# Seven block products instead of eight for an FFN down projection, with the operand sums made on VectorE

## The reference, cut to what matters

```python
hf = rmsnorm(x, norm_ffn_g)
x = x + (jax.nn.silu(hf @ w_gate) * (hf @ w_up)) @ w_down   # w_down: 2816 x 1024
...
return rmsnorm(x, norm_final_g)
```

## Time and profile before

| | |
|---|---|
| runs | 1137.77 us median of 3 (1137.57 to 1142.76) |
| profiled execution | 1141.42 us, span from first to last instruction 1139.6 us |
| busy share of the span | PE 98%, VectorE 62%, ScalarE 51%, GpSimd 13% |
| granted TensorE clock | 0.996 of full speed over the span |
| chain that ended last | PE 83% of the span |
| DMA | 193.96 MB, mean 170 GB/s |

### The profile page before, as it was taken

How to read it: one execution, slowest core, us unless ns; L and a number is a source line. 1 busy time by engine, 2 the same in 40 slices (tenths; PEclk the granted TensorE clock), 3 DMA queues, 4 the chain that set the end, 5 groups by cost and what they waited for, 6 DMA issues and landing times.

```text
span 1139.6 us, 17781 instructions
## 1 busy us (share of the span) xinstructions
PE 1112.0 (98%) x7033; PEld 984.8 (86%) x7033; DVE 707.6 (62%) x997; ACT 583.6 (51%) x767; POOL 142.6 (13%) x105
## 2 busy tenths in 40 slices
PE   8899999999998999999999999999999999999997
PEld 7767888888887888888888999898899989999996
DVE  5764565565668646565656878566587566554554
ACT  5565544444579554444455546455555346443443
POOL 3543300000265240000030000000000011000001
PEclk9999999999999999999999999999999999999999
DMA  7917565555442236556545654436643545656552
GB/s 216 306 54 186 182 198 188 200 190 184 118 137 88 98 111 222 191 186 201 189 156 185 204 171 149 132 128 223 203 159 120 185 148 160 221 175 194 189 172 89
DMA packets 138782, 193.96 MB, mean 170 GB/s; under 512 B 7147, under 2 KB 112840, under 8 KB 138716
## 3 DMA queue, kind: packets, MB, share of 16 engines
q1 hardware_dynamic: 126796, 181.92, 48.4%
q10 hardware_dynamic: 11312, 11.05, 3.6%
q0 software_dynamic: 608, 0.08, 0.1%
HBM read 191.90 MB, written 6.37 MB: 174 GB/s over the span
## 4 chain that ended last, share of the span: by engine, by line
PE 83%; ACT 6%; DVE 5%; issue 2%; DMA 2%; POOL 0%; ACTq 0%; DVEq 0%; POOLq 0%
PE psum L548 20%; PE psum L549 20%; PE psum L550 20%; PE psum L709 11%; PE psum L710 5%; ACT arena L1552 3%; PE psum L637 2%; ACT whi L1566 2%; DVE wlo L2125 1%; DMA raw<-in_a_w_in 1%; PE psum L1264 1%; PE psum L668 1%; PE psum L1237 1%; DVE arena L2566 1%; DMA raw<-in_b_w_o 0%
## 5 line engine op out<-in xcount | busy, mean ns | idle before, releaser
L1566 ACT ACTIVATE whi<-raw 128x2048 fp32r<-128x2048 f32 (+2 forms) x174 | 325.9, 1875 | 255.5 <-PE psum L550 172.5
L2125 DVE TENSOR_TENSOR wlo<-raw,whi 128x2048 fp32r<-128x2048 f32 (+1 forms) x149 | 337.5, 2267 | 184.1 <-ACT whi L1566 183.2
L548 PE MATMUL psum<-xA,whi 128*128 128x256 f32 x840 | 239.8, 285 | 2.7 <-DVE wlo L2125 1.7
L549 PE MATMUL psum<-xA,whi 128*128 128x256 f32 x840 | 237.6, 283 | 0.0
L550 PE MATMUL psum<-xA,wlo 128*128 128x256 f32 x840 | 237.5, 283 | 0.0
L1535 POOL TENSOR_TENSOR wlo<-raw,whi 128x288 fp32r<-128x288 f32 (+3 forms) x56 | 112.6, 2037 | 793.8 <-ACT whi L1566 793.5
L709 PE MATMUL psum<-xA,whi 128*128 128x512 f32 x512 | 183.0, 400 | 0.0
L548 PEld LDWEIGHTS psum<-xA,whi 128*128 128x128 f32 x840 | 160.3, 191 | 6.0 <-DVE wlo L2125 3.2
L549 PEld LDWEIGHTS psum<-xA,whi 128*128 128x128 f32 x840 | 160.4, 191 | 0.7
L550 PEld LDWEIGHTS psum<-xA,wlo 128*128 128x128 f32 x840 | 160.4, 191 | 0.1
L548 PE MATMUL psum<-whi,xC 128*128 128x512 f32 (+1 forms) x384 | 149.2, 389 | 1.1 <-DVE xC L2439 1.1
(11 more groups left out here) (269 smaller groups left out, 1339.7 us busy)
## 6 DMA issues: line engine op xcount, KB each, us to landing
raw<-in_w_in SPq DMA_DIRECT2D x42, 1024.0 KB, 4.9
raw<-in_mlp_w_up SPq DMA_DIRECT2D x32, 1024.0 KB, 5.4
raw<-in_mlp_w_down SPq DMA_DIRECT2D x32, 1024.0 KB, 4.8
raw<-in_w_gate SPq DMA_DIRECT2D x11, 1024.0 KB, 5.1
raw<-in_w_up SPq DMA_DIRECT2D x11, 1024.0 KB, 5.2
raw<-in_w_down SPq DMA_DIRECT2D x11, 1024.0 KB, 4.8
raw<-in_a_w_in SPq DMA_DIRECT2D x6, 1024.0 KB, 7.1
raw<-in_a_w_o SPq DMA_DIRECT2D x4, 1024.0 KB, 4.7
```

Source lines behind the costliest of these rows:

```text
L548: nc.tensor.matmul(out, lh, rh, start=start, stop=False, skip_group_check=skip)
L549: nc.tensor.matmul(out, lh, rl, start=False, stop=False, skip_group_check=skip)
L1566: nc.scalar.activation(whi[c % N_SPLIT][:, 0:n], raw[c % N_RAW][:, 0:n], ACT.Copy).then_inc(hi_sem, 1)
L2125: V.tensor_tensor(wlo[c % N_SPLIT][:, 0:n], raw[c % N_RAW][:, 0:n], f(whi[c % N_SPLIT][:, 0:n]), ALU.subtract).then_inc(lo_sem["dve"], 1)
```

## The change

The eight block products of d_0 to d_9 become seven products of sums (the scheme of Strassen and Winograd); d_10 keeps its eight. The MLPs of the first two layers stay as they are.

- **Operands.** VectorE makes four sums of the down weights (`wsum`, 4 × 512 columns) and four of the hidden features (4 × 128). With the three weight blocks that are used plain, the weights' high and low parts are 7 × 512 = 3584 columns a turn, in buffers of their own (`down_split`, two turns' worth); the hidden features' are 7 × 128 = 896. The weight sums of d_{p+1} are made in turn p, "a turn ahead".
- **Buffers.** d chunks leave the ring of `raw` buffers and have two of their own (`down_raw` and a part of `arena`). g and u chunks alternate in the two `raw` buffers. The loading order is unchanged, but d0 is loaded earlier, behind the last chunk of the layer before, and each d load waits for the low part of the d chunk two before.
- **Banks.** M1, M5, M6 and M7 collect in banks 4 to 7, M2, M3, M4 in banks 3, 2, 1. Gate and up sums both use bank 0 from g2 on, so g_{p+1} waits for the product of turn p and u_{p+1} for the scaled gate of p+1.
- **Order on TensorE.** g_{p+1}; M1, M6, M7; u_{p+1}; M5, M2, M3, M4.
- **The end.** `seven_sums` puts M1 and M5 to M7 together into `hres`, before `residual_add`.

The core of the diff:

```diff
@@ PE
-            def ffn_down(c, lo_count, h_count, j2, start, last):
-                ...
+            def seven_products(s, p, order, loop=None, start=False, closing=None, part=None):
+                ...
+                if part in (None, 0):
+                    pe.wait_ge(down_low_raw, count(lambda x: whole_count(s, x)))
+                    pe.wait_ge(down_low_sum, count(lambda x: sums_count(s, x)))
+                    pe.wait_ge(hidden_low, count(lambda x: whole_count(s, x)))
+                ...
+                for m in order:
+                    b, x, w = seven[m]
+                    ins = three(psum[:, b, :], xh[:, x, :], xl[:, x, :], wh[:, w, :], wl[:, w, :], start, True, True)
+                    ...
+            wide_step("g1", 5, low[index["ffn.g1"]], None)
+            wide_step("u1", 7, low[index["ffn.u1"]], None)
+            open_seven("F")
+            pe.wait_ge(gate_scaled, 2)
+            seven_products(2, 0, ("M2", "M3", "M4", "M1", "M5", "M6"), None, True, None, 0)
+            pe.wait_ge(hidden_step, hidden_count(2, 1, 1))
+            seven_products(2, 0, ("M7",), None, True, None, 1)
+            def ffn_turn(p, loop=None, closing=None, cut_at=3):
+                ...
+                wide_step(f"g{p + 1}", 0, count(lambda x: low[index[f"ffn.g{x + 1}"]]), (hidden_step, count(free_up)))
+                seven_products(2, p, SEVEN[:cut_at], loop, False, closing, 0)
+                wide_step(f"u{p + 1}", 0, count(lambda x: low[index[f"ffn.u{x + 1}"]]),
+                          (gate_scaled, count(lambda x: x + 2)))
+                seven_products(2, p, SEVEN[cut_at:], loop, False, closing, 1)
+            ...
+            ffn_turn(8)
+            ffn_turn(9, None, "F", 2)
+            four_products(2, "F")
@@ SP
+            def freed(cs, r=None):
+                users = [prev_raw[c] for c in cs]
+                if chunks[users[0]]["down"]:
+                    semaphore, values = down_low_raw, [whole_count(*chunks[x]["down"]) for x in users]
+                else:
+                    semaphore, values = lo_sem[chunks[users[0]]["lo"]], [low[x] for x in users]
+                sp.wait_ge(semaphore, values[0] if r is None else along(values, r))
@@ ACT
+            def ffn_step(p, loop=None):
+                hidden_copy(2, p, loop)
+                down_high(2, p + 1, ahead_of(loop))
+                gate_silu(p + 1, ahead_of(loop))
+                for w in "gu":
+                    ... split of ffn.{w}{p + 2}
+            gate_silu(0)
+            down_high(2, 0)
@@ DVE
+            def weight_sums(s, p, loop=None):
+                ...
+                dve.wait_ge(raw_sem[raw_of[c]], along(at, loop[1]) if loop else at[0])
+                b = raw_bufs[raw_of[c]].rearrange("p (a n) -> p a n", n=512)
+                step(1, V.tensor_tensor(wsum[:, 0:2, :], b[:, 0:1, :].to_broadcast([P, 2, 512]), b[:, 1:3, :], ALU.add))
+                step(2, V.tensor_tensor(wsum[:, 2, :], b[:, 1, :], wsum[:, 1, :], ALU.add))
+                V.tensor_tensor(wsum[:, 3, :], b[:, 3, :], wsum[:, 2, :], ALU.add).then_inc(down_sum, 1)
+            def ffn_step(p, loop=None):
+                product(p, loop)
+                hidden_sums(2, p, loop)
+                if p < NF - 2:
+                    weight_sums(2, p + 1, ahead_of(loop))
+                hidden_rest(2, p, loop)
+                if p < NF - 2:
+                    sum_low(2, p + 1, ahead_of(loop))
+                gate_scale(p + 1, ahead_of(loop))
+                raw_low(2, p + 1, ahead_of(loop))
+                for w in "gu":
+                    ... low part of ffn.{w}{p + 2}
+            gate_scale(0)
+            weight_sums(2, 0)
+            sum_low(2, 0)
+            raw_low(2, 0)
+            for p in range(2):
+                ffn_step(p)
+            ... (turns 2 to 7 in a loop, 8 and 9)
+            product(NF - 1)
+            hidden_rest(2, NF - 1)
+            seven_sums("F")
             final_norm()
```

More of the change, by code:

```diff
@@ L1326, in wide_step @@
                 ins.then_inc(gu_full, 1)
-            def ffn_down(c, lo_count, h_count, j2, start, last):
[L1329 to L1339, removed]
+            for p in range(NF):
+                for w in range(2):
+                    chunk_done[index[f"ffn.{'gu'[w]}{p}"]] = (gu_full, 2 * p + w + 1)
+            wide_step("g0", 4, low[c0], None, late_tile("F"))
+            wide_step("u0", 6, low[c0 + 1], None)
             out = open_bank("F.rs", 3)
@@ L1371, in _ @@
+            ffn_turn(1)
+            with pe.Fori(0, 3) as r:
+                for q in range(2):
+                    ps_ = [2 + 2 * y + q for y in range(3)]
+                    ffn_turn(ps_[0], (ps_, r))
+            ffn_turn(8)
+            ffn_turn(9, None, "F", 2)
+            four_products(2, "F")
         @block.sync
@@ new lines, in hidden_copy, with count @@
+            def hidden_copy(s, p, loop=None):
+                def count(at):
+                    return along([at(x) for x in loop[0]], loop[1]) if loop else at(p)
+                last = p == down_steps[s] - 1
+                act.wait_ge(hidden_step, count(lambda x: hidden_count(s, x, 1 if last else 4)))
+                if p >= 2:
+                    act.wait_ge(seven_done, count(lambda x: sums_count(s, x - 2)))
+                v = slice(0, 512) if last else slice(P, 1024)
+                nc.scalar.activation(hidden_hi[p % 2][:, v], hidden[:, v], ACT.Copy).then_inc(hidden_high, 1)
@@ L1571, in split_to @@
                     c = next_split[0]
-                    split_one(c, landed[c], chunk_done[c - N_SPLIT] if c >= N_SPLIT else None)
+                    if not chunks[c]["down"]:
+                        split_static(c)
                     next_split[0] += 1
@@ L2102, in _ @@
-            ffn_static(NF - 1)
+                    ps_ = [2 + 2 * y + q for y in range(3)]
+                    ffn_step(ps_[0], (ps_, r))
+            for p in (8, 9):
+                ffn_step(p)
+            first_copy("F")
+            hidden_copy(2, NF - 1)
             final_norm()
@@ new lines, in hidden_rest, with seven_sums, scaled @@
+            def hidden_rest(s, p, loop=None):
+                at = [whole_count(s, x) for x in (loop[0] if loop else (p,))]
+                dve.wait_ge(hidden_high, along(at, loop[1]) if loop else at[0])
+                v = slice(0, 512) if p == down_steps[s] - 1 else slice(P, 1024)
+                V.tensor_tensor(hidden_lo[p % 2][:, v], hidden[:, v], f(hidden_hi[p % 2][:, v]),
+                                ALU.subtract).then_inc(hidden_low, 1)
+            def seven_sums(n):
+                def scaled(b, half, src, scale, then=None):
+                    h = hres[:, b, 512 * half:512 * half + 512]
+                    run(V.scalar_tensor_tensor(h, src, scale[:, b:b + 1], h, ALU.mult, ALU.add), then)
+                run(V.tensor_scalar(minus_scale, late_scale, -1.0, None, ALU.mult))
+                dve.wait_ge(*read[f"{n}.M1"])
+                dve.wait_ge(*full[f"{n}.M6"])
+                run(V.tensor_tensor(wsum[:, 1, :], psum[:, 6, :], wsum[:, 0, :], ALU.add), read[f"{n}.M6"])
+                scaled(1, 1, wsum[:, 0, :], late_scale)
+                dve.wait_ge(*full[f"{n}.M7"])
+                run(V.scalar_tensor_tensor(wsum[:, 2, :], psum[:, 7, :], -1.0, wsum[:, 1, :], ALU.mult, ALU.add), read[f"{n}.M7"])
+                scaled(1, 0, wsum[:, 1, :], minus_scale)
+                dve.wait_ge(*full[f"{n}.M5"])
+                scaled(1, 0, psum[:, 5, :], late_scale)
+                scaled(0, 0, psum[:, 5, :], late_scale, read[f"{n}.M5"])
+                scaled(0, 0, wsum[:, 2, :], minus_scale)
+                scaled(0, 1, wsum[:, 2, :], late_scale)
@@ new lines, in product @@
+            def product(p, loop=None):
+                dve.wait_ge(gu_full, count(lambda x: 2 * x + 2, p, loop))
+                dve.wait_ge(silu_done, count(lambda x: x + 1, p, loop))
+                if p:
+                    dve.wait_ge(hidden_low, count(lambda x: whole_count(2, x - 1), p, loop))
+                V.tensor_tensor(hidden[:, 0:512], psum[:, (6, 7)[p] if p < 2 else 0, :], gate_buf,
+                                ALU.mult).then_inc(hidden_step, 1)
+                dve.wait_ge(hidden_step, count(lambda x: hidden_count(2, x, 1), p, loop))
```

364 lines of the change are left out of this document (231 added, 133 removed).

## The result

The changed kernel takes 1214.77 us (median of 4 runs, 1210.79 to 1220.45), the kernel before 1138.67 (4 runs): ratio 1.0654, 95% interval 1.062 to 1.0689, so 6.5% slower. The forecast was 1197 us, with a range of 1171 to 1211. The time lies 3.8 us above the range and 18 us above the forecast. The profiled execution took 1220.45 us, the longest of the four.

A forecast was written before the change was run, and what follows sets the result against it. VectorE's turn, with a late load of d in it, was taken to bound the kernel: beginning +11.3, eight turns +45.7, tail +2.5, last turn −0.3, together +59.2 on 1137.8, so 1197 us; 80% range 1171 to 1211.

The forecast's parts named there:

- What bounds it, and by which chain: Eight middle FFN turns: VectorE's chain, waiting for a late load of d, sets 22.7 us a turn, 5.7 longer than before.
- The beginning and the end: FFN's ends: gate scale 0 to product 1 25.4 us (+11.3); product 9 to end of span 33.7 (tail +2.5).
- TensorE's gain of 0.23 us a matmul: Ten d steps: three of 24 matmuls dropped in each, 30 × 0.228 = 6.8 us; TensorE's turn could be 16.30 us.
- The chain without the load: VectorE's middle turn from d's landing, without product and hidden sums: 14.57 us.
- L: Each middle turn: time from the end of low u to the landing of d, taken as 8.1 us, ends 5.3 and 9.3.
- the pair: Loads of g0 and u0, landing 2.9 us apart, the second 5.9 after issue; put a third load at 8.1 to 8.8.
- A: Rival, middle turns: d comes in time, turns of 16.3 us, +7.7 us in all, 1145.5 us; chance 0.06.
- B: Rival, whole FFN: TensorE stays the bound, VectorE's added work is hidden, −4.3 us, 1133.5 us; chance 0.03.
- C: Rival, middle turns: TensorE's clock falls, +79 us, 1276 us, chance 0.03; harmless form: half rate after each stall, then recovery.

The follow-up runs named there:

- d_early: The changed kernel with each load of d issued a turn earlier, ahead of the loads of g and u; 1154.07 us, ratio 1.0122.
- d_mid: The changed kernel with the load of d between those of g and u instead of behind u; 1184.73 us, ratio 1.038.
- old_places: d_early with xC and arena put back at their addresses in the kernel before; 1148.13 us, ratio 1.0065.
- half_d: The changed kernel with loads of d2 to d9 that bring only half the columns; 1206.75 us, ratio 1.0569.
- only_arena: The kernel before with arena alone allocated behind all other buffers; 1140.97 us, ratio 1.0019.
- g2_first: begin_end with g2 ahead of d0 on TensorE, then d0, u2, all of d1 and g3; 1140.77 us, ratio 1.0013.
- begin_end: old_places with VectorE, ScalarE and TensorE reordered at both ends of the FFN; 1143.78 us, ratio 1.0019.

## Why the prediction came out as it did

**What bounds it, and by which chain: right.** VectorE's turn with a load of d in it, asked for behind the wait for u's buffer. It is shown by d_early and d_mid, which change nothing but the place of that load and take turns of 16.25 and 20.7 us in place of 24.15.

**The beginning and the end: right.** 25.3 against 25.4 us, and 33.9 against 33.7. The gap ahead of d0 was 8.8 us (8.4 forecast). TensorE's gain of 0.23 us a matmul was real as well: its turn is 16.39 us in d_early and 16.32 in old_places (1003.62 to 1019.94), in place of 16.98.

**The chain without the load: right.** The turn shown above gives 24.05 − 9.4 = 14.65 us, the mean of the eight 24.15 − 9.55 = 14.60, against 14.57.

**L: the step that failed, by its size.** The prediction put it at "8.1, the lower edge of what the pair gives". Measured: 9.55 on the mean, above even the 9.3 that it named as the upper end. That is 1.45 us a turn too little, and over eight turns the 11.6 us by which the middle of the FFN is longer than forecast. 1.1 us of it is u, which landed 7.0 us after its issue, not 5.9 as the second of a pair in the earlier trace rows. The rest is the step from u's landing to d's, 2.5 us where 2.2 was taken. I had priced the pair from a burst that had no third load behind it, and had then taken the lower end, because d's rows are longer pieces. No run shows a gain from them, since the third place took 9.0 us with d in it and 8.9 with u. The same pair, taken at its upper edge, pointed to 8.8. half_d shows that half of d's bytes cost 24.15 − 22.77 = 1.4 us a turn.

**The missing term.** The move of `xC` to another address was in the diff and had no term in the sum. It costs 0.13 us in each of the 32 MLP turns, 4.2 us ahead of the FFN. The seven products do not read `xC`; their hidden blocks lie in `xB`, which has moved as well. With the buffers at their new places TensorE's turn is 0.07 us longer (16.39 in d_early, 16.32 in old_places), which costs nothing in the changed kernel, since its middle turns are VectorE's. So 11.7 us of the 18 by which the forecast was short lie in the FFN and about 4.2 in this term; some 2 are left unexplained. The growth adds up likewise: 70.9 + 4.2 = 75.1 us, against the 76.1 between the medians. The profiled execution lost 8.2 us ahead of the FFN, some 4 more than this term. That part varies by itself. The first 100 us, in old_places and then in only_arena:

```profile
0.00:100.00 100.00, 92.34 (x603) 75.44 (x604) 66.33 (x196) 62.19 (x128) 41.49 (x33) 0.98 0.67 198
```

```profile
0.00:100.00 100.00, 86.16 (x541) 69.56 (x542) 61.03 (x185) 57.79 (x114) 41.51 (x33) 0.91 0.59 178
```

TensorE got through 603 and 541 matmuls in that stretch, at clocks of 0.98 and 0.91. Gate scale 0 came at 954.60 in old_places and at 964.93 in only_arena, though both have the fast pace in the MLPs and do the same work ahead of the FFN, but for the early load of d0. A comparison of two single spans carries this error; the ruler from gate scale 0 doesn't (181.5 us in the kernel before, 181.6 in only_arena).

**The rivals.** A (d in time) was forecast at +7.7 us; d_early, which makes it true, has an FFN of 190.0, +8.5. B has its sign in d_early's middle turns, where the gate scale starts 0.8 us after M1 (1040.78 and 1040.00). It also needed VectorE to be hidden at the beginning; even g2_first, which reorders for exactly that, comes only to even, with 4.8 us of idle TensorE left. C came true in its harmless form, in every middle turn: the clock stands at 0.50 to 0.62 in the stretch of 5 to 6.5 us around the restart, and nothing is lost, since VectorE's product waited for TensorE once, 0.2 us. In the beginning of begin_end, where TensorE is the bound, the same fall was not harmless: the matmuls behind it took 2.7 us more.

## What to carry to other kernels

Before an operation is moved forward in an engine's program, look up when its data is asked for: a load with a free buffer still stands behind the wait of the load ahead of it in the queue. Price a load in a burst by its place there, from the nearest burst of the same length, and take the upper edge if there is none. Read every line of the diff for addresses as well as for operations, and compare single profiles from a mark just ahead of the change.

## What the hardware showed that I had not expected

- The pace of 512-column matmuls depends on where the buffer with their stationary blocks lies: 0.2278 us with `xC` at the old place or 80 KB a partition below it, 0.2330 with it behind the small buffers. Two places are fast and two slow; the reason is open.
- A two-input VectorE instruction on SBUF that starts during a GpSimd instruction of the same kind waits for its end: 0.29 us became 4.66.
- Idle time of 4.8 us in pieces of up to 1.8 left the granted clock at 1.00 over 120 us (g2_first). With 6.0 us, of which one piece of 4.7, it was 0.97 (begin_end).
- Three loads of 1 MB issued within 2.7 us land 5.3, 7.0 and 9.0 us after their issues. The third takes as long with u in that place (8.9), and 6.8 to 7.6 with half the bytes, which does not bring the second in sooner (6.9).
